# Identity products on TensorE ahead of its waits, and the next expert's gather split around the scatter

## The reference, cut to what matters

```python
h = x
h = h + gla_mixer(rms_norm(h, attn_norm[0]), ...)          # gated linear attention, 4 heads
h = h + swiglu(rms_norm(h, ffn_norm[0]), ...)              # "f1", hidden 2816
kv = rms_norm(h, kv_norm) @ sb_w_kv
h = h + stick_breaking_mixer(rms_norm(h, attn_norm[1]), k, v, ...)   # 8 heads
h = h + moe_swiglu(rms_norm(h, ffn_norm[1]), ...)          # top 2 of 8 experts, hidden 3584
h = rms_norm(h, final_norm)
# second block
x = h + mixer(rms(h, norm_mix_g), ...)   # 8 softmax heads ("fox"), 4 mLSTM heads, 4 HGRN heads
x = x + conv_glu(rms(x, norm_ffn_g), ...)                  # "f2", hidden 2816
```

## Time and profile before

| | |
|---|---|
| time, median of 3 runs | 1910.81 us (1909.76 to 1911.23) |
| the profiled execution: its own time, its span | 1909.01 us, 1907.3 us |
| busy share of the span | PE 95%, DVE 73%, ACT 60%, POOL 7% |
| mean granted PE clock over the span | 0.968 of full |
| HBM read | 476.72 MB, 251 GB/s over the span |
| stage of the eight experts, from the timeline | about 488 to 1488 us |

### The profile page before, as it was taken

The page is one execution under the profiler, slowest core; times in us unless marked ns, Lnnn a source line. Parts: engine busy times, 40 slices in busy tenths (PEclk is TensorE's granted clock), DMA queues, the critical chain, the costliest instruction groups (busy, mean ns, idle before and its releaser), DMA issues.

```text
span 1907.3 us, 25401 instructions
## 1 busy us (share of the span) xinstructions
PE 1818.5 (95%) x9810; PEld 1567.7 (82%) x9810; DVE 1400.8 (73%) x1160; ACT 1148.1 (60%) x949; POOL 142.7 (7%) x140
## 2 busy tenths in 40 slices
PE   7979999988999999999999999999999898879999
PEld 6769999887788888888888888888888787769998
DVE  6455455545788888898889888898888675367775
ACT  6334344473676777767777767777677454535553
POOL 6030000000000000000000000000000125520000
PEclk9999999998999999999999999999999898589999
DMA  6554665431898998998989989999899332215551
GB/s 205 176 136 155 199 195 178 158 133 67 303 377 313 380 378 307 386 363 326 381 310 375 369 321 376 345 346 379 314 377 348 122 123 82 89 45 177 198 179 65
DMA packets 248515, 479.31 MB, mean 251 GB/s; under 512 B 15919, under 2 KB 84297, under 8 KB 248409
## 3 DMA queue, kind: packets, MB, share of 16 engines
q1 hardware_dynamic: 247545, 476.49, 69.9%
q10 hardware_dynamic: 864, 1.31, 0.2%
HBM read 476.72 MB, written 1.05 MB: 251 GB/s over the span
## 4 chain that ended last, share of the span: by engine, by line
PE 89%; DVE 4%; ACT 3%; issue 2%; POOL 1%; DMA 0%; SPq 0%; ACTq 0%; DVEq 0%; POOLq 0%
PE bank L1874 27%; PE bank L1876 27%; PE bank L1875 27%; PE bank L2170 2%; PE bank L2200 1%; PE bank L1840 1%; DVE wl L439 1%; PE bank L2339 1%; DVE xT L1246 0%; PE bank L1960 0%; ACT wh L432 0%; POOL wl L439 0%; PE bank L2340 0%; POOL xTl L725 0%; PE bank L2150 0%
## 5 line engine op out<-in xcount | busy, mean ns | idle before, releaser
L1874 PE MATMUL bank<-wh,xTh 128*128 128x512 f32 x1568 | 624.6, 398 | 15.3 <-POOL xTl L725 5.9
L1876 PE MATMUL bank<-wh,xTl 128*128 128x512 f32 x1568 | 615.3, 392 | 0.0
L1875 PE MATMUL bank<-wl,xTh 128*128 128x512 f32 x1568 | 614.7, 392 | 0.0
L1488 DVE TENSOR_TENSOR wl<-raw,wh 128x2048 fp32r<-128x2048 f32 x224 | 512.1, 2291 | 97.0 <-ACT wh L1016 95.1
L1016 ACT ACTIVATE wh<-raw 128x2048 fp32r<-128x2048 f32 x224 | 429.2, 1918 | 125.4 <-PE bank L1876 125.4
L1874 PEld LDWEIGHTS bank<-wh,xTh 128*128 128x128 f32 x1568 | 297.6, 190 | 77.1 <-POOL xTl L725 6.7
L1876 PEld LDWEIGHTS bank<-wh,xTl 128*128 128x128 f32 x1568 | 297.0, 189 | 63.5
L1875 PEld LDWEIGHTS bank<-wl,xTh 128*128 128x128 f32 x1568 | 297.7, 190 | 59.7 <-issue 0.2
L439 DVE TENSOR_TENSOR wl<-raw,wh 128x2048 fp32r<-128x2048 f32 x110 | 254.5, 2330 | 74.9 <-ACT wh L432 73.1
L1874 PE MATMUL bank<-xTh,wh 128*128 128x256 f32 x1024 | 292.7, 286 | 9.6 <-issue 5.4
L1875 PE MATMUL bank<-xTl,wh 128*128 128x256 f32 x1024 | 291.6, 285 | 0.0
(11 more groups left out here) (380 smaller groups left out, 1450.9 us busy)
## 6 DMA issues: line engine op xcount, KB each, us to landing
raw<-in_moe_w_up SPq DMA_DIRECT2D x112, 1024.0 KB, 7.6
arena<-in_moe_w_gate SPq DMA_DIRECT2D x96, 1024.0 KB, 7.2
raw<-in_moe_w_down SPq DMA_DIRECT2D x96, 1024.0 KB, 6.9
raw<-in_w_up SPq DMA_DIRECT2D x22, 1024.0 KB, 5.2
raw<-in_moe_w_gate SPq DMA_DIRECT2D x16, 1024.0 KB, 7.1
arena<-in_moe_w_down SPq DMA_DIRECT2D x16, 1024.0 KB, 7.2
raw<-in_gla_w_in SPq DMA_DIRECT2D x12, 1024.0 KB, 5.4
raw<-in_w_in SPq DMA_DIRECT2D x12, 1024.0 KB, 6.0
```

What stands on the lines that cost most here:

```text
L1488: V.tensor_tensor(wl[:, s, :], moe_raw(c)[0], wh[:, s, :].bitcast(F32), ALU.subtract).then_inc(lo_moe, 1)
L1874: T.matmul(o, xh, yh, start=first, stop=False)
L1875: T.matmul(o, xh, yl, start=False, stop=False)
L1876: return T.matmul(o, xl, yh, start=False, stop=last)
```

## The change

A helper `keep(label, n)` takes the bank of a label that comes next anyway and multiplies the 128x128 identity by itself n times into it, in float32; nothing reads that result, and the next real user of the bank overwrites it. It stands ahead of second-tile (and some first-tile) transposes of n1 to n5, after the norms of f1 and f2, ahead of the stick-breaking queries, between router and positions, and ahead of the first softmax head. In the experts the second half of the gather moves from before `last_down` to between the scatter's halves, and into the other bank; DVE and ACT handle its read-out later; PE waits for the split of the next expert's input by halves; and the last expert gathers nothing.

```diff
@@ act @@
-            def xg_hi(value):
-                for half in range(2):
-                    act.wait_ge(sg("moe_xg"), value + half)
-                    V.activation(xgh[half of it], xg[half of it], ACT.Copy).then_inc(sg("moe_xh"), 1)
-            xg_hi(1)
+            def xg_hi(half, value):
+                act.wait_ge(sg("moe_xg"), value)
+                V.activation(xgh[half of it], xg[half of it], ACT.Copy).then_inc(sg("moe_xh"), 1)
+            for half in range(2):
+                xg_hi(half, half + 1)
...
-                        if tail:
-                            xg_hi(at(4, 2 * i + 3))
+                        if tail and (more_follow or i == 0):
+                            xg_hi(0, at(4, 2 * i + 3))
+                        if (kind, j, k) == ("d", NEJ - 1, 1) and (more_follow or i == 0):
+                            xg_hi(1, at(4, 2 * i + 4))
@@ dve @@
+                    last = i == 1 and not more_follow
...
-                            gates_now(at(2, i + 1))
-                            onehot(at(2, i + 1), at(2, i + 2))
-                        if (kind, j, k) == ("d", NEJ - 2, 1):
-                            for half in range(2):
-                                gather_out(half, bank[7] if half == 0 else bank[(NEJ * (i + 1)) % 2], at(4, 2 * i + 3 + half))
-                            for half in range(2):
-                                xg_lo(half, at(4, 2 * i + 3 + half))
+                            if not last:
+                                gates_now(at(2, i + 1))
+                                onehot(at(2, i + 1), at(2, i + 2))
+                        if (kind, j, k) == ("d", NEJ - 2, 1) and not last:
+                            gather_out(0, bank[7], at(4, 2 * i + 3))
+                            xg_lo(0, at(4, 2 * i + 3))
                     for half in range(2):
                         ...                                   # eyl of both halves
+                    weights_lo(UC - 2)
+                    if not last:
+                        gather_out(1, bank[(NEJ * (i + 1) + 1) % 2], at(4, 2 * i + 4))
+                        xg_lo(1, at(4, 2 * i + 4))
                     for q in range(4):
                         ...                                   # four additions to h
-                    weights_lo(UC - 2)
                     weights_lo(UC - 1)
@@ pe @@
+            def keep(label, n):
+                ps = take(label)
+                for _ in range(n):
+                    T.matmul(ps[:, 0:P], ident[:, :], ident[:, :], start=True, stop=True)
+
-            def transposes(n, ready, parts=order(False)):
+            def transposes(n, ready, parts=order(False), idle={}):
                 for t, half in parts:
+                    if (t, half) in idle:
+                        keep((n, t, half), idle[t, half])
                     ready(t, half)
...
-            norm("n1")
+            norm("n1", {(1, 0): 17})
+            keep(("f1", 0, "g"), 7)
             x_split()
...
-            norm("n2")
+            norm("n2", {(0, 0): 7, (1, 0): 7})
...
             tm(("sv", 1))
+            keep(("sq", 0), 8)
             x_split()
...
-            norm("n3")
+            norm("n3", {(1, 0): 15})
...
             done(ins, "lg")
+            keep("pos", 9)
             pe.wait_ge(sg("rt_sel"), 1)
...
                     def gate_up(b, kind, j):
                         for half in range(2):
+                            if kind == "g" and j == 0:
+                                pe.wait_ge(sg("moe_xl"), at(4, 2 * i + 1 + half))
...
-                    pe.wait_ge(sg("moe_xl"), at(4, 2 * i + 2))
                     for j in range(NEJ):
...
-                    pe.wait_ge(sg("moe_oh"), at(2, i + 2))
+                    last = i == 1 and not more_follow
                     pe.wait_ge(sg("moe_ohT"), at(2, i + 1))
-                    gather(0, bank[7])
-                    gather(1, bank[(NEJ * (i + 1)) % 2])
+                    if not last:
+                        pe.wait_ge(sg("moe_oh"), at(2, i + 2))
+                        gather(0, bank[7])
                     last_down()
-                    pe.wait_ge(sg("moe_xg"), at(4, 2 * i + 4))
+                    if not last:
+                        pe.wait_ge(sg("moe_xg"), at(4, 2 * i + 3))
+                    else:
+                        pe.wait_ge(sg("moe_ghot"), at(2, i + 1))
                     pe.wait_ge(sg("moe_yl"), at(4, 2 * i + 1))
                     scatter(0, 0, bank[7])
                     scatter(1, 0, bank[4])
+                    if not last:
+                        gather(1, bank[(NEJ * (i + 1) + 1) % 2])
                     pe.wait_ge(sg("moe_yl"), at(4, 2 * i + 2))
                     scatter(0, 1, bank[5])
                     scatter(1, 1, bank[6])
...
-            norm("n4")
+            norm("n4", {(0, 0): 24, (1, 0): 7})
...
+            keep(("s", 0), 14)
             pe.wait_ge(sg("qk_n"), 2)
...
-            norm("n5")
+            norm("n5", {(1, 0): 18})
+            keep(("f2", 0, "g"), 7)
             x_split()
             ffn("f2")
```

More of the change, by code:

```diff
@@ L1033, in _ @@
             act.wait_ge(sg("more_ready"), 1)
-            def xg_hi(value):
-                for half in range(2):
-                    act.wait_ge(sg("moe_xg"), value + half)
-                    V.activation(xgh[:, 4 * half:4 * half + 4, :], xg[:, 4 * half:4 * half + 4, :], ACT.Copy).then_inc(sg("moe_xh"), 1)
-            xg_hi(1)
+            def xg_hi(half, value):
+                act.wait_ge(sg("moe_xg"), value)
+                V.activation(xgh[:, 4 * half:4 * half + 4, :], xg[:, 4 * half:4 * half + 4, :], ACT.Copy).then_inc(sg("moe_xh"), 1)
+            for half in range(2):
+                xg_hi(half, half + 1)
             def experts(at, more_follow):
@@ L1865, in _, with norm @@
             n_x = [0]
-            def norm(n):
+            def norm(n, idle={}):
                 n0 = n_xn[0]
                 n_xn[0] += TT
-                transposes(n, lambda t, half: pe.wait_ge(sg("xn_ready"), n0 + t + 1))
+                transposes(n, lambda t, half: pe.wait_ge(sg("xn_ready"), n0 + t + 1), idle=idle)
             def mm3(o, xh, xl, yh, yl, first, last):
```

## The result

| | time, median (lowest to highest) | ratio to before, 95% interval |
|---|---|---|
| before | 1911.01 us (1909.76 to 1911.23, 4 runs) | |
| after | 1890.89 us (1890.01 to 1891.14, 4 runs) | 0.9895 [0.9878, 0.9912] |
| forecast | 1888.5 us, 1876 to 1898 | |

The change takes 20.1 us off. The profiled execution of after took 1890.74 us with a span of 1889.0, 18.3 less than the one of before.

The account below looks back on a forecast made before the run. PE bounds the kernel (89% of the span's last-ending chain), through its idle time and half-clock pace. Terms summed to 21.7 us off the profiled 1909.0, giving 1887.3; the forecast was 1888.5 us, range 1876 to 1898.

Parts of the forecast that it names:

- Seven expert ends: At expert ends with a follower, the moved gather covers PE's 1.10 us idle time; net 0.7 us each, 4.9 in all.
- wait of 0.55 us: At seven expert ends, PE waits 0.55 us after the gate's first half for DVE's late xg_lo.
- Last expert: In the eighth expert the gather goes, saving 3.5 us, while the wait of 1.1 us stays; bounds 2.9 and 3.5.
- n1, n2, n5: At these three norms full clock replaces half clock, saving 2.2, 1.5 and 3.4 us.
- n3 and router: Transposes and router products gain 4.1 us, full clock is lost within the router, the fill gives 1.7 back: 2.4 us.
- first expert: Ahead of its gate, PE may start on half 0, whose split ends sooner than half 1's: 0.8 us.
- n4: Fill ahead of its transposes gains 1.6 us; half clock in one execution of three eats it; 1.1 taken, bounds 1.6 and -4.9.
- Heads: Softmax heads: faster front, then 2.8 us idle beside half-array work loses the clock, which stays down; 1.9 us saved.
- Rival 1: The clock holds through the softmax heads, some 15 us more saved, 1874 us; chance 12%.
- Rival 3: Identity products don't hold the clock and fills run at half: slower, 1913 us, up to 1925; chance 4%.
- Rival 4: The fills work only in part, two or three norms still fall: 1891 to 1896 us; chance 14%.
- signs that the prediction named for its stretches: Clock 1.00 from 137 to 150, in n2, and from 1705 through f2; router between; heads 0.50 for most.

Follow-up runs that it names:

- e8: The kernel before with only the eighth expert's gather left out: 1908.13 us, ratio 0.9990.
- e7: The kernel after with its fills multiplying only 64 of the identity's 128 rows: 1898.51 us, ratio 0.9942.
- e3: The kernel after with 11 more identity products in the idle time ahead of the first softmax head's transposes: 1882.24 us, ratio 0.9856.
- e5: The kernel after with the 11 products of e3 and ACT's two weight pieces taken apart, at the third and sixth head: 1880.38 us, ratio 0.9844.
- e10: The kernel after with 16 identity products on 64 of 128 rows ahead of the fourth softmax head's transposes: 1894.10 us, ratio 0.9912.
- e1: The kernel after without any identity products, only the expert changes: 1898.37 us, ratio 0.9941.
- e9: The kernel after with 16 identity products on all 128 rows ahead of the fourth softmax head's transposes: 1890.65 us, ratio 0.9897.

## Why the prediction was right, and where it was not

- **Seven expert ends: 4.9 forecast, 8.2 measured.** The step that failed is the placement of the second half's split on ACT and DVE. Counted from the first gather's start I had `xg_lo` done at 14.2 us (740.05 - 725.88) and PE there at 13.6; it was done at 13.63 (732.01 - 718.38), PE came at 13.70. Most of the 0.54 us between was there before DVE's weight piece: I had ACT's second `eyh` done at 9.02 (734.9 - 725.88), and it was done at 8.66 (727.04 - 718.38). From `eyl` to gather_out I had 2.95, and it took 2.80. Part of both is that I put whole durations end to end, where the rows overlap by some 0.1 us each (on DVE 727.74 + 2.28 is 730.02, and the next starts at 729.94; on ACT 724.56 + 1.90 is 726.46, and the next starts at 726.37). About 0.25 us is more than that: ACT's weight piece began at 6.18 (724.56 - 718.38), and in my placement, with its durations taken off, at 6.43. So the wait of 0.55 us that I charged seven times never came, and each end gave the whole 1.1. The margin is 0.07 us: that no wait at all came is luck.
- **Last expert: 3.5 forecast, 3.5 between the rows, 3.6 in e8.** The wait of 1.1 stayed.
- **n1, n2, n5: 2.2, 1.5, 3.4 forecast; 2.0, 1.5, 2.7 measured.** Full clock throughout; right in mechanism and nearly in size.
- **n3 and router: 2.4 forecast, 1.7 measured up to the first gather; first expert: 0.8 forecast, 0.6 measured.** As forecast, full clock was lost within the thin router products (465.3) and the fill ran on into half: it took 4.08 us and gave 1.6 back where the term had 1.7. The transposes and router products gained 2.6 in place of 4.1, the position products 0.7. The first gate's wait shrank from 2.22 us to 1.59, which is right in mechanism; the gathers between were 0.15 slower.
- **n4: 1.1 forecast, -0.2 measured.** It was the case that I had given one execution in three: idle 1.08, a microsecond of scatters, idle 1.17, and the clock falls at the fill. Of the seven profiled kernels that have this order and a fill of 24 (in e7 on 64 rows) it fell in six and held in one, e3. The chance was wrong, not the mechanism.
- **Heads: 1.9 forecast, 1.4 measured at the front.** The idle time ahead of the first transposes was forecast as 2.8 and is 2.77 us; the clock fell there (1612.1) and stayed down. e3 and e5 turn this reading into a result: with the gap filled the heads run at full clock. The argument also named the 64-row work beside the gap; that such work loses the clock by itself is false by e5. That it didn't lift the clock in this stage held again in after and e10.
- **Behind the heads: 0 forecast, -3.6 measured.** Here the sum has no term at all. Half clock ended at 1666.7 in after and at 1668.0 in before, though all work came 19 us sooner. In before it rose behind the mLSTM heads' first 64-row pairs, and the rest of that stage ran at full clock but for 3.4 us; in after the same pairs (1644.88 on) did not lift it, so that the whole stage and w2's first dense products ran at half. The prediction left out that the end of half clock need not move with the work. In e1, e5 and e9 it stands elsewhere again; what decides whether the pairs lift it is open.

Rival 1 had the right mechanism under a condition that the change did not meet. It was worth less than its 15 us: 8.7 in e3's median (n4's clock held there too), and 10.8 in the stage itself with e5, since what follows falls again. Rival 3 is out: the products held the clock, and zeros did so as well. Rival 4 came true in part, for n3 and n4. The signs that the prediction named for its stretches, the scatter's wait and the last gather were all seen; the one that failed is the wait of 0.5 us seven times. The total, 2.4 us above the forecast, is right partly by luck, since two errors of 3.3 and 3.6 us cancel. The sum also took 1.2 us back in for the median where its own figure was 1.8; with that it would have said 1889.1.

The Trainium skill's "TensorE: Matmul & The Clock Gate", section "What's actually happening", ties the clock to how busy PE is. If busy is read as the profile's busy time, e10 disagrees for lifting: PE busy for 7.20 of 7.20 us and 21.70 of 22.30 at 0.50. By that rule e9 and e10 would have been the same; they differ by the rows alone. For holding, e5 agrees: 36.26 of 36.80 us busy at 1.00, 64-row work included.

## What to carry over

Where the tensor engine is the bound, look for its half-clock stretches first, and then at the one idle time ahead of each: products that nobody reads, put there, hold the pace, and their values may be zeros. They are cheap as long as they end inside the idle time; once the clock is down, products on all rows brought it back where the same number on half of them did not, and a fill caught by the fall costs twice. When two engines' lists are laid side by side, take distances between starts, not durations: here rows overlap by 0.1 us each, and a margin of 0.07 us decided that no wait came.

## What the runs showed of the hardware that I had not expected

- With 64 of 128 rows, products one after another hold the full clock (n1 in e7, heads in e5) but didn't lift it (16 products and 17 us of heads in e10, 24 products in n4 of e7); with 128 rows the same number lifts it (e9, from 0.50 to 1.00 within 5.5 us).
- Behind 64-row products that go side by side, one head's on each half of the rows, the clock rose in six of the profiled kernels (before at 1668.0, e10 at 1656.3) and stayed at half in six others (after from 1644.88 on).
- Products of zeros hold it like any (1892.48 against 1890.89 us).
- Idle times of only 1.0 to 1.2 us were followed by half clock (e3 at 1619.79, e5 at 1627.80, after at 1471.87), though not always (e3 had 1.20 us ahead of 1473.27 and kept full clock), while in the dense layers 2.18 us did not lead to it. What decides between them is open.
